# Reading samples' new retention states as high and low fp32r parts with two query columns

## The reference, cut to what matters

```
S_new = S * g + k^T v          # S is 256 x 512, one per sample, head and layer
o     = q S_new                # 512 values for one query q of 256
```

## Time and profile before

| | |
|---|---|
| median of 3 runs | 2779.52 us (2766.94 to 2781.74) |
| the profiled execution | span 2784.4 us |
| PE busy | 93% of the span |
| DVE, POOL, ACT busy | 52%, 50%, 21% |
| granted TensorE clock, mean over the span | 0.964 of 2.4 GHz |

### The profile page before, as it was taken

One profiled execution on the slowest core, in us unless ns is written; L12 is line 12 of the kernel. 1 busy time (PEld: TensorE's weight loads), 2 busy tenths in 40 slices (PEclk: granted clock), 3 DMA queues, 4 the chain that ended last, 5 costly groups with the idle time before them and its releaser, 6 DMA issues.

```text
span 2784.4 us, 53033 instructions
## 1 busy us (share of the span) xinstructions
PE 2598.1 (93%) x20388; PEld 2551.3 (92%) x20388; DVE 1435.8 (52%) x1644; ACT 594.0 (21%) x825; POOL 1404.3 (50%) x845
## 2 busy tenths in 40 slices
PE   7999999987889999999999999899888899999997
PEld 7998989987889989999998989898788899999997
DVE  6656454587764553223256453646876745431333
ACT  2303030316161121001112121213161611110111
POOL 4252526244456656666653525252455566566664
PEclk9999999999999999999999989999999999999999
DMA  4435353422222222232236252524222222222222
GB/s 156 168 122 164 121 160 118 159 72 68 65 78 89 92 76 92 86 96 91 88 131 199 89 189 91 191 92 163 62 73 72 74 92 89 76 89 93 91 87 87
DMA packets 113015, 298.52 MB, mean 107 GB/s; under 512 B 11681, under 2 KB 12449, under 8 KB 112865
## 3 DMA queue, kind: packets, MB, share of 16 engines
q1 hardware_dynamic: 60480, 199.78, 22.4%
q10 hardware_dynamic: 52384, 96.56, 10.4%
HBM read 255.92 MB, written 40.38 MB: 106 GB/s over the span
## 4 chain that ended last, share of the span: by engine, by line
PE 72%; DVE 14%; DVEq 7%; issue 3%; ACT 2%; ACTq 1%; DMA 1%; POOL 0%; POOLq 0%
PE proj L299 63%; PE aux L469 3%; DVEq L1011 2%; DVE scratch L829 2%; PE aux L460 1%; PE aux L450 1%; DVEq L828 1%; DVE scratch L775 1%; PE aux L417 1%; DVE scratch L913 1%; DVE scratch L917 1%; DMA scratch<-v_rows 1%; DVE scratch L780 1%; ACTq L1269 1%; DVE scratch L638 1%
## 5 line engine op out<-in xcount | busy, mean ns | idle before, releaser
L285 POOL TENSOR_SCALAR w_high<-w_raw 128x1024 fp32r<-128x1024 f32 (+3 forms) x420 | 438.0, 1043 | 1294.5 <-PE proj L299 1290.2
L287 POOL TENSOR_TENSOR w_low<-w_raw,w_high 128x1024 fp32r<-128x1024 f32 (+3 forms) x420 | 965.9, 2300 | 62.2 <-issue 1.5
L299 PE MATMUL proj<-x_high,w_high 128*128 128x260 f32 x4096 | 855.2, 291 | 97.0 <-DVE scratch L895 34.6
L299 PE MATMUL proj<-x_high,w_low 128*128 128x260 f32 x4096 | 841.5, 288 | 0.0
L299 PE MATMUL proj<-x_low,w_high 128*128 128x260 f32 x4096 | 840.4, 287 | 0.0
L299 PEld LDWEIGHTS proj<-x_high,w_high 128*128 128x128 f32 x4096 | 650.4, 194 | 109.9 <-issue 52.5
L299 PE MATMUL proj<-split_scratch,w_high 128*128 128x260 f32 x4000 | 655.4, 286 | 43.5 <-DVE scratch L802 17.1
L299 PEld LDWEIGHTS proj<-x_high,w_low 128*128 128x128 f32 x4096 | 648.3, 193 | 0.0
L299 PEld LDWEIGHTS proj<-x_low,w_high 128*128 128x128 f32 x4096 | 647.7, 193 | 0.0
L299 PEld LDWEIGHTS proj<-split_scratch,w_high 128*128 128x128 f32 x4000 | 556.4, 191 | 51.0 <-DVE scratch L802 18.3
L299 PE MATMUL proj<-split_scratch,w_low 128*128 128x260 f32 x2000 | 406.2, 285 | 0.0
(11 more groups left out here) (142 smaller groups left out, 2086.5 us busy)
## 6 DMA issues: line engine op xcount, KB each, us to landing
w_raw<-in_wstream SPq DMA_DIRECT2D x252, 512.0 KB, 3.3
scratch<-in_sret ACTq DMA_DIRECT2D x64, 512.0 KB, 6.3
out_ret_s<-scratch ACTq DMA_DIRECT2D x64, 512.0 KB, 6.4
w_raw<-in_wstream SPq DMA_DIRECT2D x72, 448.0 KB, 3.2
w_raw<-in_wstream SPq DMA_DIRECT2D x48, 384.0 KB, 3.1
scratch<-v_rows ACTq DMA_DIRECT2D x64, 256.0 KB, 5.3
w_raw<-in_wstream SPq DMA_DIRECT2D x48, 320.0 KB, 2.9
out_ret_p<-scratch ACTq DMA_DIRECT2D x8, 512.0 KB, 3.1
```

Of the source, the lines that this page charges most:

```text
L285: pool.tensor_scalar(WH[:, j, w], WR[:, j, w], 1.0, 0.0, ALU.mult, ALU.add)
L287: pool.tensor_tensor(WL[:, j, w], WR[:, j, w], WH[:, j, w].bitcast(F32), ALU.subtract).then_inc(s["w_split"], 1)
L299: m = pe.matmul(out, wt[:, w, blk * P:(blk + 1) * P], x[xi], start=first and n == 0, stop=last and n == 2)
```

## The change

ACT copies each half d of a new state, rounded to fp32r, into a new buffer `SSH` (`s_high`); DVE subtracts that from the state into a new buffer `SSL` (`s_low`). PE reads out both parts, each with two moving columns, the high and the low part of the query, which lie in the split query buffers already: 4 x 2 x 2 = 16 fp32r products for a sample in place of 8 fp32 products. The readouts of high and low query stand side by side in PSUM, and two DVE instructions add them. There is one `SSH` and one `SSL` for all samples, so ACT's copy for sample b waits for the readout of the same half of sample b - 1. ACT now waits for `new_state(b)` within iteration b, and issues the store there; before, it issued it one iteration later. A setting of the DMA's scratch memory becomes smaller to make room.

```
@@ PE
                     def sample_out(b):
-                        pe.wait_ge(s["s_new"], hh * NS + (b + 1))
-                        for e in range(VT):
-                            for d in range(KT):
-                                m = pe.matmul(AUX[:, BANK_SO, e * NS + b:e * NS + b + 1],
-                                              SS[b % SRING][:, d, e * P:(e + 1) * P],
-                                              QF[:, d, SEQ + b:SEQ + b + 1],
-                                              start=b == e == d == 0, stop=d == KT - 1,
-                                              skip_group_check=True)
-                        m.then_inc(s["so_done"], 1)
+                        for d in range(KT):
+                            pe.wait_ge(s["s_low"], hh * (NS * KT) + (b * KT + d + 1))
+                            for e in range(VT):
+                                for n, part in enumerate((SSH, SSL)):
+                                    m = pe.matmul(AUX[:, BANK_SO, 2 * (e * NS + b):2 * (e * NS + b + 1)],
+                                                  part[:, d, e * P:(e + 1) * P], q_sample(d, b),
+                                                  start=b == e == d == n == 0, stop=d == KT - 1 and n == 1,
+                                                  skip_group_check=True)
+                            m.then_inc(s["so_done"], 1)
@@ DVE
+                    def state_low(b):
+                        for d in range(KT):
+                            dve.wait_ge(s["s_high"], hh * (NS * KT) + (b * KT + d + 1))
+                            tt(SSL[:, d, :], SS[b % SRING][:, d, :], SSH[:, d, :].bitcast(F32), ALU.subtract
+                               ).then_inc(s["s_low"], 1)
+
                     gate(0)
                     new_state(0)
                     gate(1)
+                    state_low(0)
                     new_state(1)
+                    state_low(1)
                     new_state(2)
                     gate(3)
+                    state_low(2)
                     new_state(3)
                     for e in range(VT):
                         attended(e)
+                        state_low(VT - 1 + e)
                         new_state(VT + e)
-                    dve.wait_ge(s["so_done"], hh * NS + NS)
-                    ts(OF[:, :, SEQ:TOK], AUX[:, BANK_SO, 0:VT * NS].rearrange("p (e b) -> p e b", e=VT),
-                       1.0, None, ALU.mult)
+                    state_low(NS - 1)
+                    dve.wait_ge(s["so_done"], hh * (NS * KT) + NS * KT)
+                    so = AUX[:, BANK_SO, 0:2 * VT * NS].rearrange("p (e b n) -> p n e b", e=VT, n=2)
+                    ts(OF[:, :, SEQ:TOK], so[:, 0], 1.0, None, ALU.mult)
+                    dve.drain()
+                    tt(OF[:, :, SEQ:TOK], so[:, 1], OF[:, :, SEQ:TOK], ALU.add)
                     dve.drain()
@@ ACT
                     for b in range(NS):
                         act.wait_ge(v_ld[b % VRING], hh * (16 * NS // VRING) + 16 * (b // VRING + 1))
-                        if b >= 2:
-                            act.wait_ge(s["s_new"], hh * NS + (b - 1))
                         A(TS[b % 2][:, 0, :], VB[:, b % VRING, :], copy, scale=KSC[:, 0, b:b + 1])
...
                             load_state(b + 1)
-                        if b:
-                            act.wait_ge(s["s_new"], hh * NS + b)
-                            act.dma_start(state(ret_s, b - 1), SS[(b - 1) % SRING]
-                                          ).then_inc(s_st[(b - 1) % SRING], 16)
+                        act.wait_ge(s["s_new"], hh * NS + (b + 1))
+                        for d in range(KT):
+                            if b:
+                                act.wait_ge(s["so_done"], hh * (NS * KT) + ((b - 1) * KT + d + 1))
+                            A(SSH[:, d, :], SS[b % SRING][:, d, :], copy).then_inc(s["s_high"], 1)
+                        act.dma_start(state(ret_s, b), SS[b % SRING]).then_inc(s_st[b % SRING], 16)
```

More of the change, by code:

```diff
@@ L147, in build @@
         KSC = sb("k_sample", [P, KT, NS])
+        SSH = sb("s_high", [P, KT, DV], F32R)
+        SSL = sb("s_low", [P, KT, DV], F32R)
         R_HEAD = 4 * KT * TOK + 2 * TT * DV + 2 * TT * DK + 2 * ST_OFF[TT]
@@ L160, in build, with q_sample @@
         o += 2 * VT * TOK
+        def q_sample(d, b):
+            return R[:, d * TOK + SEQ + b:(KT + d) * TOK + SEQ + b + 1:KT * TOK]
         KDH, KDL = rview(o, TT, DK), rview(o + TT * DK, TT, DK)
@@ L215, in build @@
                  "rope_done qk_high qk_low st_high st_low aux_mm aux_free kv_high kv_low "
-                 "vs_st dec_ld trig_ld silu_g t_mul s_new so_done gn_sum centred gn_sq gn_sd var_rd og_full og_high "
+                 "vs_st dec_ld trig_ld silu_g t_mul s_new s_high s_low so_done gn_sum centred gn_sq gn_sd var_rd og_full og_high "
                  "og_low sfin_st sq_mm state_ld xc_full xc_high xc_low lam_exp gate_r gate_i th_full d_full "
@@ L1176, in one_head @@
                             act.wait_ge(s_st[n % SRING], hh * (16 * SUSES[n % SRING]) + 16 * (n // SRING + 2))
-                            act.wait_ge(s["so_done"], hh * NS + (n + 1))
+                            act.wait_ge(s["so_done"], (hh * NS + (n + 1)) * KT)
                             load_state(b + 1)
-                        if b:
-                            act.wait_ge(s["s_new"], hh * NS + b)
-                            act.dma_start(state(ret_s, b - 1), SS[(b - 1) % SRING]
-                                          ).then_inc(s_st[(b - 1) % SRING], 16)
+                        act.wait_ge(s["s_new"], hh * NS + (b + 1))
[4 more added lines that the diff above has]
+                        act.dma_start(state(ret_s, b), SS[b % SRING]).then_inc(s_st[b % SRING], 16)
                         if b in (1, 2, 3):
                             silu((0, 1, 3)[b - 1])
-                    act.wait_ge(s["s_new"], hh * NS + NS)
-                    act.dma_start(state(ret_s, NS - 1), SS[(NS - 1) % SRING]
-                                  ).then_inc(s_st[(NS - 1) % SRING], 16)
                     half = VT // 2
@@ L1446 @@
                 conv_s=(DEPTH, P, LT, CW - 1, NS))
-    nc = bacc.Bacc("TRN2", target_bir_lowering=False, num_devices=1)
+    nc = bacc.Bacc("TRN2", target_bir_lowering=False, num_devices=1, dynamic_dma_scratch_size=1024)
     arrays, aps = {}, {}
```

## The result

The changed kernel takes 2936.52 us (median of 4 runs, 2920.02 to 2945.45) against 2777.94 for the kernel before (4 runs on the same chip): a ratio of 1.0572, 95% interval 1.0529 to 1.0614. The medians lie 158.6 us apart, the spans of the profiled executions (2939.8 and 2784.4) 155.4. The mean granted clock of the whole span goes from 0.964 to 0.930.

What follows compares the result with a forecast made beforehand. PE, busy 93%, was taken to bound the kernel. Undisturbed stretch 30.8 plus waits, loads and tail 11.1 plus clock 9 gave 50.9 us against 33.8: 17.1 a head, 137 us in eight, 2916 us (2840 to 2990).

Steps and rivals of the forecast that it cites:

- The passes bring nothing: PE's readouts: sixteen fp32r passes replace sixteen fp32 passes at about 0.11 us each, so no gain.
- (2): Readout on PE: fp32r passes cost half of the fp32 ones, 58 us less than forecast, 2858 us; chance 0.07.
- (4): Readout on PE: the fp32r weight load is hidden entirely, so the kernel is not slower; chance 0.05.
- Six waits of 1.6 us: PE waits for DVE's queued subtraction before the readouts of samples 0 and 2 to 6: 9.5 us a head.
- Samples 1 and 7 covered: Readouts of samples 1 and 7 don't wait for the subtraction; if uncovered, each costs up to 1.6 us.
- rival 3: DVE's subtraction takes 1.78 us, not 0.69: 6.5 us a head more, 2968 us; chance 0.09.
- State loads: ACT issues loads of old states later, so they land late: 1.2 us a head, bounds 0 and some 4.
- The clock, 9 us: In the readout stretch the granted clock falls to half in every head, for half the time: 9 us a head.
- rival 1: In the readout stretch the clock holds wherever it holds now; only waits are paid: +65 us, 2845; chance 0.17.
- the bound of 18.3: Upper bound of the clock term: everything from readout 2 to readout 7 at half clock, 18.3 us a head.
- The tail: After the last readout: one more small DVE instruction and a drain, 0.4 us a head.

Runs made afterwards that it cites:

- the run of the waits with the old passes: Changed kernel with the fp32 one-column readout of before, no ACT copies, and unused DVE subtractions that the readouts wait for: 2926.76 us, ratio 1.0538.
- the run with the dense filling: Changed kernel plus 12 unread passes of 260 columns ahead of the readouts of samples 0 and 2 to 6: 2854.55 us, ratio 1.0284.
- The filled pauses: Changed kernel plus 12 unread PE passes ahead of six readouts a head, in two runs: 260 columns, 2854.55 us; 2 columns, 2951.37 us.
- The exchanged operands: Kernel before with masked queries as readout weights and the state's 512 columns moving in fp32, rows brought back to columns: 2791.46 us, ratio 1.0048.
- the last run: Kernel before with the state as moving operand and sample 7 read ahead of both state products: 2771.81 us, ratio 0.9977.

## Why the prediction was right

The forecast was 2916 (2840 to 2990), slower; the time is 2936.52. The waits came about by the mechanism forecast; the clock fell further than forecast, and not for the waiting alone. Point by point:

- **The passes bring nothing.** 1024 passes stay, 0.11 us apart. The rivals that a pass costs half (2) or is hidden (4) are dead, and the run of the waits with the old passes shows it from the other side. That an fp32 product costs two passes holds for such thin ones alone (last point of this document).
- **Six waits of 1.6 us.** 48 waits, 75.0 us for the weight load, 1.56 each: 9.4 us a head for a term of 9.5. They stand at samples 0 and 2 to 6, behind the instructions named. Putting the subtractions ahead of these took half of them away.
- **Samples 1 and 7 covered.** In the changed kernel, yes. For sample 1 the reason held only by luck: its subtractions run beside POOL and take 2.1 to 4.2 us for two, not 1.4, and what covers them is gate 3 at half clock. In the run with the dense filling, at nearly full clock, they take 4.2 in every head and the readout's second half waits there, 1.1 us each time. So the mechanism of rival 3 exists, at one sample instead of six.
- **State loads, 1.2 us.** Measured 0. DVE's `new_state`, which waited 24.1 us for loads in the earlier trace rows, waits for none in the profile after; with a stretch half as long again the loads have more time. The mechanism is there all the same: with the readouts' waits gone and the copies kept, it waits 31.1 us for them.
- **The clock, 9 us.** It falls in every head, so rival 1 is dead, but the term was mis-sized. 53.5 measured less 41.5 at full clock is 12.0, and 13.1 if the 1.1 at sample 1 that the changed kernel doesn't have is taken off. I had set half of the bound of 18.3, and it is about seven tenths.
- **The tail.** DVE waits for the last readout as predicted, 36.2 us in eight times at L789.

With the measured terms, 0.2 being what is left of the 41.5 for the tail when the 1.1 is taken off, the sum is 30.8 + 9.4 + 0.2 + 13.1 = 53.5, 19.7 a head over 33.8, where I had 17.1: 157 us instead of 137. In the kernel before the clock cost 33.8 - 30.8 = 3.0 of this; it is now more than four times that. About half of the loss is waiting (75 us), the other half the clock (10.1 us a head more than before, 81 in eight).

What was not right is the picture of the clock: I took the waiting for its cause. The filled pauses show that it matters what PE does in them, since the clock also fell after thin passes without a pause. The exchanged operands show that the readout's own thin passes have a part: without them the clock holds in every head, where before it held in two, and it holds even through the pauses of the last run. Pauses may have a part beside thin passes. With the dense filling, the six heads at 0.96 lose the clock once each, 1.2 to 1.7 us after the wait at sample 1. In the kernel before, PE waits for a new state five times, once each in five of the six heads that lose the clock, 2.0 to 3.1 us ahead of the fall:

```profile
PE aux L469 <- DVE scratch L747: 1.9, 5, 0.8
```

How pauses and thin passes share the fall in the changed kernel is not shown.

## What to carry to other kernels

Where a change puts an operation on another engine between producer and consumer, ask what stands ahead of it in that engine's order: a subtraction of 0.69 us cost 1.6 because it was queued behind an instruction that waits for the very engine that waits for it. A pass that loads 128 columns of weights for one or two moving columns costs the same in fp32 as in fp32r here, so splitting gains nothing there, while the exchange of the operands gave passes that held the clock. After taking a wait away, read the windows again, clock and all: twice here the next engine in line was late at once.

## What the runs showed of the hardware

- Eight stretches with PE busy 415.49 of 418.53 us in all ran at granted clocks of 0.64 to 0.82, with two-column passes as filling, and once the clock fell there with PE busy without a break for 14 us. With 260-column passes in the same places they ran at 0.96 to 1.00, and with 512 moving columns in all readouts at 1.00 in every head.
- At half clock a thin pass costs twice as well: the readout's passes are 0.11 us apart at full clock and 0.21 at half, though they hold only two columns. I read it as the weight load following the granted clock. The Trainium skill (TensorE: Matmul & The Clock Gate, "LDWEIGHTS (loading the stationary operand)") gives a load by its columns alone, 128 / 1.2 = 107 ns as an estimate; the distance between passes agrees with that at full clock and not at half; the records of the loads themselves last 0.19 us and 0.33.
- The same subtraction of 128 x 512 took 0.68 us alone and up to 2.88 beside POOL's subtraction of 128 x 1024 (2.63 us long). The Trainium skill (SBUF — State Buffer, "Who interferes with whom") has VectorE and GpSimd share a pair of ports under an exclusive lock; with that the trace agrees: the eleven slow subtractions of the changed kernel each end 0.54 or 0.55 us after an instruction of POOL that ran beside them.
- An fp32 product has two records on PE. With one moving column they are 0.11 us apart, as fp32r passes are. With 512 (the two runs with the state as the moving operand) they are 0.43 us apart, where fp32r passes of 512 columns (`final_state`) are 0.23 apart. So thin passes cost the same in fp32 and in fp32r here, and wide ones do not.
